# Eight attention streams that start zero, one or two steps apart

## The reference

```
s = (jnp.einsum('bqhd,bqnsd->bqhns', q_blk, kg).astype(jnp.float32) * (E ** -0.5)
     - slopes[None, None, :, None, None] * dist)
...
p = masked_softmax(s.reshape(B, QB, H, -1), mask.reshape(B, QB, H, -1)).reshape(s.shape)
return jnp.einsum('bqhns,bqnsd->bqhd', p.astype(q_blk.dtype), vg)
...
o = g[..., 0:1] * o_cmp + g[..., 1:2] * o_sel + g[..., 2:3] * o_win
```

## Time and profile before

| | |
|---|---|
| time, median of 3 runs | 5168.52 us (5166.04 to 5174.38) |
| the profiled execution | 5176.21 us, span 5174.4 us |
| mean granted TensorE clock | 0.878 |
| TensorE busy | 4328.4 us, 84% |
| VectorE busy | 1970.4 us, 38% |
| ScalarE busy | 1205.4 us, 23% |
| POOL busy | 1208.5 us, 23% |

### The profile page before, as it was taken

How to read it: one execution, slowest core, us unless ns; L and a number is a source line. 1 busy time by engine, 2 the same in 40 slices (tenths; PEclk the granted TensorE clock), 3 DMA queues, 4 the chain that set the end, 5 groups by cost and what they waited for, 6 DMA issues and landing times.

```text
span 5174.4 us, 48896 instructions
## 1 busy us (share of the span) xinstructions
PE 4328.4 (84%) x19930; PEld 3443.9 (67%) x19930; DVE 1970.4 (38%) x2449; ACT 1205.4 (23%) x1535; POOL 1208.5 (23%) x588
## 2 busy tenths in 40 slices
PE   5646799999589999899999779989886989766577
PEld 4435688888456666678888658867674868654456
DVE  6882412222532223222222373244534444155432
ACT  2433221111212223321111232121212131122201
POOL 3543322222311112322222322221111121100043
PEclk9778899999679999899999889989896989755588
DMA  3001011111100000111111122221112111200042
GB/s 113 25 25 53 29 49 49 49 47 47 53 17 17 17 17 29 65 41 49 46 48 49 45 74 98 98 70 56 49 60 75 44 61 56 91 30 9 17 179 82
DMA packets 77417, 275.15 MB, mean 53 GB/s; under 512 B 8836, under 2 KB 9480, under 8 KB 72712
## 3 DMA queue, kind: packets, MB, share of 16 engines
q1 hardware_dynamic: 77192, 272.02, 15.5%
HBM read 219.55 MB, written 52.43 MB: 53 GB/s over the span
## 4 chain that ended last, share of the span: by engine, by line
PE 70%; DVE 19%; ACT 4%; POOL 3%; DMA 2%; issue 1%; SPq 0%; DVEq 0%; POOLq 0%; ACTq 0%
PE ps L339 44%; PE ps L367 7%; DVE ca L688 3%; PE ps L1954 2%; PE ps L1285 2%; DVE t L453 2%; PE ps L1269 2%; PE ps L1966 2%; PE ps L2810 1%; PE ps L1287 1%; PE ps L1961 1%; DVE n L2827 1%; PE ps L2003 1%; DVE n L2834 1%; DVE ps L512 1%
## 5 line engine op out<-in xcount | busy, mean ns | idle before, releaser
L285 POOL TENSOR_TENSOR wlo<-wraw,whi 128x1024 fp32r<-128x1024 f32 x301 | 726.7, 2414 | 2656.5 <-ACT whi L277 2650.5
L339 PE MATMUL ps<-xhi,whi 128*128 128x512 f32 x3280 | 1065.3, 407 | 233.8 <-DVE xlo L475 75.9
L339 PE MATMUL ps<-xlo,whi 128*128 128x512 f32 x3280 | 1043.3, 400 | 0.0
L339 PE MATMUL ps<-xhi,wlo 128*128 128x512 f32 x3280 | 1038.9, 399 | 0.0
L339 PEld LDWEIGHTS ps<-xhi,whi 128*128 128x128 f32 x3280 | 620.8, 194 | 375.3 <-DVE xlo L475 87.7
L277 ACT ACTIVATE whi<-wraw 128x1024 fp32r<-128x1024 f32 x301 | 318.9, 1060 | 2108.1 <-PE ps L339 1725.1
L339 PEld LDWEIGHTS ps<-xlo,whi 128*128 128x128 f32 x3280 | 636.7, 194 | 139.3
L339 PEld LDWEIGHTS ps<-xhi,wlo 128*128 128x128 f32 x3280 | 634.5, 193 | 138.8
L512 DVE TENSOR_TENSOR ps<-ps,t 128x1024 f32<-128x1024 f32 x161 | 198.4, 1232 | 1081.7 <-PE ps L339 1079.9
L367 PE MATMUL ps<-xhalf,whi 128*128 128x512 f32 x1024 | 374.3, 449 | 0.0
L339 PE MATMUL ps<-xhalf,whi 128*128 128x512 f32 x1024 | 286.3, 403 | 33.0 <-DVE xhalf L475 21.2
(11 more groups left out here) (479 smaller groups left out, 4911.9 us busy)
## 6 DMA issues: line engine op xcount, KB each, us to landing
wraw<-in_w_dram SPq DMA_DIRECT2D x301, 512.0 KB, 3.6
g_keep<-gates SPq DMA_DIRECT2D x64, 256.0 KB, 2.4
gb<-g_keep SPq DMA_DIRECT2D x32, 512.0 KB, 3.6
p_keep<-stage SPq DMA_DIRECT2D x30, 512.0 KB, 2.9
x_keep<-x SPq DMA_DIRECT2D x12, 1024.0 KB, 3.8
x<-x_keep SPq DMA_DIRECT2D x12, 1024.0 KB, 8.3
x<-in_x_dram SPq DMA_DIRECT2D x4, 1024.0 KB, 11.7
n<-p_keep SPq DMA_DIRECT2D x8, 512.0 KB, 5.4
```

What stands on the lines that cost most here:

```text
L285: ge.own().tensor_tensor(K.lo(c), K.raw[:, c % NRAW, :], K.hi(c).bitcast(F32), SUB).then_inc(*K.G(("lo", c)))
L339: done = mm(into[a][:, h, :], wt, x[h], start=(i == 0 and j == 0), stop=(i == n - 1 and j == 2), skip_group_check=True)
```

## The change

Each stream gets 0, 1 or 2 empty steps in front, (4 x kind + h) mod 3, on TensorE, VectorE and ScalarE alike. For kind 0 these are 0, 1, 2, 0, and for kind 1 they are 1, 2, 0, 1. The instructions are the same ones.

```diff
+def attend_streams(stream):
+
+    return [in_turn(wait_steps((4 * kind + h) % 3), stream(kind, h)) for kind, h in STREAMS]
...
-    weave(*(attend_tensor(pe, K, R.nsa, kind, h, rings[2 * h + kind]) for kind, h in STREAMS))
+    weave(*attend_streams(lambda kind, h: attend_tensor(pe, K, R.nsa, kind, h, rings[2 * h + kind])))
...
-    weave(*(attend_vector(ve, K, H, R.nsa, kind, h) for kind, h in STREAMS))
+    weave(*attend_streams(lambda kind, h: attend_vector(ve, K, H, R.nsa, kind, h)))
...
-    weave(*(attend_scalar(se, K, R.nsa, kind, h) for kind, h in STREAMS), results_back_scalar(se, K, R))
+    weave(*attend_streams(lambda kind, h: attend_scalar(se, K, R.nsa, kind, h)), results_back_scalar(se, K, R))
```

## The result

| | before | after |
|---|---|---|
| time, median of 20 runs each | 5168.98 us (5153.56 to 5181.86) | 5178.98 us (5174.00 to 5186.52) |
| ratio | | 1.0019 (95%: 1.0012 to 1.0027) |
| span of the profiled execution | 5174.4 us | 5178.2 us |

The change costs 10 us, 0.19%. The forecast was 6 us of gain; the measured time lies above the range's end of 5175.

The account below looks back on a forecast made before the run. Levels were taken as bound by a chain from engine to engine, partly by slow TensorE. Stretch: 87.3 + 203.6 + 6.3 = 297.2 us, less 4 for the clock, against 299.2: 6 us gained, 5162.5 us; range 5138 to 5175.

Parts of the forecast that it names:

- The stretch: From the first score eviction to the end of ScalarE's last copy; 299.2 us before, forecast at 297.2 - 4 us.
- the clock term: Over the stretch, TensorE at the higher clock for part of the time: half of 8 us taken, 4 us gained.
- the sum at clock 0.50: All levels plus the tail with TensorE at 1.2 GHz throughout: 297.2 us, 2.0 less than the 299.2 before.
- What bounds the stretch: In the attention levels, a chain from engine to engine and partly a slow TensorE; the end runs through ScalarE's casts.
- The walk through level 6: Long streams A to D and short ones E to H timed step by step: 53.3 us in place of 60.3.
- Levels 1 to 3: VectorE bounds level 1, taken as 18.3 us; TensorE bounds levels 2 and 3, at 26.0 and 30.5 us.
- Cost 1: On TensorE, scores lose their pairs in the array halves: 1.28 us for a lone 384-column score, 1.71 for 512 columns.
- the second rival: On TensorE, about 112 more changes of array height cost time; from 0.15 us each the kernel takes 5179; chance 0.10.
- my sign for this rival: A score behind a value product seen later than 2.3 us would show that changes of array height cost.
- the row on the value products: Profile row before the change: 17.1 us of value products at 100% busy on TensorE did not raise the clock.
- My first rival: Mixed work releases TensorE's clock, 40 to 50% of the stretch at 2.4 GHz: 28 us gained, 5140 us; chance 0.20.

Follow-up runs that it names:

- e3: The changed kernel with value products of 128 columns in place of 64: 5149.71 us, timed once, stretch 277.8 us at clock 0.64.
- e1: The changed kernel with every score multiplied over 128 rows, two heads summed: 5133.59 us, timed once, stretch 257.6 us at clock 0.75.
- e7: The kernel before with value products of 128 columns in place of 64: 5140.28 us, ratio 0.9946 to before, stretch 270.1 us.
- e4: The changed kernel with offsets by pairs of heads, so that scores keep their pairs: 5158.13 us, ratio 0.9974 to before, stretch 296.3 us.

## Why the prediction was wrong

The stretch was to take 293.2 us and took 308.0. Of these 14.8 us, 4 are the clock term, and 10.8 are the sum at clock 0.50, 297.2 against 308.0.

- **What bounds the stretch**: right. The chain through the engines, the second chunk's wait (1.74 us, unchanged in the new order) and the end through the casts are all in the profile after.
- **The walk through level 6**: right in shape. Evictions of first chunks after, on VectorE:

```profile
4774.93 0.69 DVE L2827 SCALAR_TENSOR_TENSOR n<-ps,n 128x512 f32<-128x512 f32 x1 [1.59 <-PE ps L2798]
4777.36 0.56 DVE L2827 SCALAR_TENSOR_TENSOR n<-ps,n 128x384 f32<-128x384 f32 x1 [1.74 <-PE ps L2798]
...
4784.99 0.69 DVE L2827 SCALAR_TENSOR_TENSOR n<-ps,n 128x512 f32<-128x512 f32 x1 [3.78 <-PE ps L2798]
...
4797.46 0.69 DVE L2827 SCALAR_TENSOR_TENSOR n<-ps,n 128x512 f32<-128x512 f32 x1 [3.56 <-PE ps L2798]
...
4807.31 0.56 DVE L2827 SCALAR_TENSOR_TENSOR n<-ps,n 128x384 f32<-128x384 f32 x1 [3.57 <-PE ps L2798]
...
4818.61 0.69 DVE L2827 SCALAR_TENSOR_TENSOR n<-ps,n 128x512 f32<-128x512 f32 x1 [3.70 <-PE ps L2798]
...
4830.55 0.69 DVE L2827 SCALAR_TENSOR_TENSOR n<-ps,n 128x512 f32<-128x512 f32 x1 [1.60 <-PE ps L2798]
```

D comes 10.06 us behind A (walk: 10.1), B at 22.5 (22.3), E at 32.4 (32.0), C at 43.7 (42.3), the next A at 55.6 (53.3). It falls behind from E on, where TensorE has runs without a break. Level by level, forecast and measured: 12.5 and 12.5; 18.3 and 18.1; 26.0 and 26.4; 30.5 and 32.7; 43.6 and 45.1; 48.5 and 51.0; 53.3 and 55.6; 58.2 + 6.3 and 66.7. In sum 297.2 and 308.0.
- **Levels 1 to 3, in part by luck**: the forecast has VectorE as the bound of level 1, and there TensorE is busy 18.05 of 18.12 us. For levels 2 and 3 it counts all of a level's work, but the streams that start late still do work of the level before: the stretch of level 2 holds 21 turns and 17.5 value blocks in place of 24 and 24. At the forecast's own prices its work is 23.0 us, and it took 26.4 with TensorE full; level 3 has 29.1 us of work and took 32.7. That is 3.4 and 3.6 us for eight lone scores each, 0.42 and 0.45 a score. Against the forecast, which counted too much work at too low a price, only 0.4 and 2.2 us of it are seen.
- **Cost 1 and the second rival**: the step that failed, and by all that the levels show the one that turned the sign, since without the clock term the sum still had 2 us of gain. I wrote "so the price is under 0.1 us", from the time of the score itself. That time could not tell, since in both orders a step of 128 rows stands ahead of the score: the first chunk is seen 2.11 us after its start before (4786.65 to 4788.76), and after too, where D's score comes behind a turn:

```profile
4782.88 2.07 PE L2798 MATMUL ps<-n 64*128 64x512 f32 x2
```

(4782.88 to 4784.99). The 2.08 us that I set beside it are of two scores of 384 columns and not of one of 512. So my sign for this rival, a score seen later than 2.3 us, stayed off while the price was there. A change costs 0.30 us, 0.60 for each lone score, spread over the score and the steps on both sides; the lone times that I had named, 1.3 and 1.7 us to the next step, are 1.58 and 2.00. My walk had 3.25 us for turn, score and value of three blocks where the profile has 3.69. Over 64 scores that is some 28 us of TensorE's work, by my estimate. Where TensorE runs without a break it lengthens the level, elsewhere a part falls into waits; that this leaves just 10.8 us is argued from the levels and not shown by a run. The rival's own figure, 5179 us, was met by luck: it stood for 0.15 us a change with all of it seen. "TensorEngine Tiling (Array Packing)" in the Trainium skill says under Key Properties that a change of the tiling mode drains TensorE; that each change costs time agrees with it, and the price is this case's.
- **The clock**: "I take half, 4 us" was 0. The clock never left 0.50, though TensorE was busy 276.5 of 308.0 us. Had I taken the row on the value products (17.1 us full and slow) for the whole mixed order, I would have forecast 297.2, still 2 us of gain. My first rival said more even work lifts the clock; e3 and e1 show that it is the kind of work: the order is the same in all three.
- **The base of the sum**: right. 297.2 us is priced at clock 0.50 throughout, so that the old order's 35 us at 2.4 GHz are given up is in it already. At one clock the old order would be longer than 299.2, by an amount that no run shows.

What stays open: how the 8.8 us split. e3 and e7 at like clock put the order with its changes of height at 7.7 us of loss; e4 gains 11.7 with half the changes, the pairs back and a clock of 0.53 in place of 0.50; but no run held the clock of the new order fixed while only the height changed.

## What to carry to other kernels

When steps of several streams are mixed, count what stood side by side before: matmuls in the two halves of the array, and bursts that lifted TensorE's clock. Before offsets are judged, give the scores the full array (128 rows): here that made the same offsets worth 23 us in place of -9, the higher clock included. Try value products of 128 columns where a block takes no longer with them; they gave 29 us in the old order and 30 in the new. And price a change of array height by the starts of the same steps with and without it: a row that has the change on both sides of the comparison cannot show it.

## What the runs showed of the hardware

- A busy TensorE is no fast one: 58.98 of 59.00 us busy at a granted clock of 0.50. "TensorE: Matmul & The Clock Gate" in the Trainium skill (Part 1) has the clock follow busy-ness; these rows do not agree with busy time alone as the measure.
- At 1.2 GHz three blocks of the value product behind a 64-row score take 1.34 us with 64 columns (0.45 each) and 1.44 with 128 in e3 (0.48 each, from 4773.29 to 4774.73): the second 64 columns cost nearly nothing and lifted the clock.
- A change between steps of 64 and of 128 rows costs about 0.30 us at 1.2 GHz (3.69 against 3.09 us for the same steps in after and e1). Two 64-row scores of 384 columns side by side in the two halves take 1.58 us together in e4, as long as one alone in after.
- VectorE's mask addition of 512 columns took 2.35 us in place of 0.69 beside a POOL subtraction, once in the stretch (timeline of after: start us, us, engine, operation):

```profile
4646.41 2.35 POOL L2885 TENSOR_TENSOR xlo<-yb,xhi 128x1024 fp32r<-128x1024 f32 x1 [143.68 <-ACT xhi L2878]
4646.95 2.35 DVE L2831 TENSOR_TENSOR n<-n 128x512 f32<-128x512 f32 x1
...
4651.91 0.69 DVE L2831 TENSOR_TENSOR n<-n 128x512 f32<-128x512 f32 x1
```

In the old order that subtraction fell into the value products (from 4653.95), where VectorE had no such addition.
